# Row-sum copies of branch b issued at weight quarters 16, 20 and 24 instead of 25, 29 and 33, and one pair of row quarters requested two weight quarters later

## The reference, cut to what matters

```python
h = rmsnorm(x, p['norm_w']) * (1 + scale) + shift
proj = h @ p['w_in']
o_a, sfa, sba = gdn_branch(qkv, z_a, gate_cols, p, s_af, s_ab)     # branch a
o_b, sfb, sbb = lru_branch(x_b, z_b, p, s_bf, s_bb, col_major)     # branch b
pa = o_a @ p['w_proj_a']
pb = o_b @ p['w_proj_b']
g_a, g_b = jnp.split(jax.nn.sigmoid(h @ p['w_gate'] + p['b_gate']), 2, axis=-1)
mixed = (g_a * pa + g_b * pb) @ p['w_out']
return x + gate * mixed, ...
```

## Time and profile before

| | us |
|---|---|
| Median of 3 runs | 1464.38 (1463.67 to 1464.54) |
| The profiled execution, its own time | 1463.94 |
| Its span on the core | 1462.2 |
| PE busy | 1441.4 (99%) |
| DVE busy | 1140.8 (78%) |
| ACT busy | 872.8 (60%) |
| POOL busy | 457.2 (31%) |

### The profile page before, as it was taken

How to read it: one execution, slowest core, us unless ns; L and a number is a source line. 1 busy time by engine, 2 the same in 40 slices (tenths; PEclk the granted TensorE clock), 3 DMA queues, 4 the chain that set the end, 5 groups by cost and what they waited for, 6 DMA issues and landing times.

```text
span 1462.2 us, 29461 instructions
## 1 busy us (share of the span) xinstructions
PE 1441.4 (99%) x11640; PEld 1385.0 (95%) x11640; DVE 1140.8 (78%) x1983; ACT 872.8 (60%) x1836; POOL 457.2 (31%) x395
## 2 busy tenths in 40 slices
PE   8999999999999999999999999999999999999997
PEld 7899999999999999999899999999999999999886
DVE  5799898888989798888957766777666847888954
ACT  6574857667484756758357676556675564453311
POOL 3032322232332223233312122212224654656310
PEclk9999999999999999999999999999999999999999
DMA  9423133332413233432515686657868899747232
GB/s 315 123 70 123 31 79 112 75 110 62 140 48 78 96 75 109 122 123 80 162 40 144 197 218 150 140 180 198 172 171 267 263 276 253 224 151 237 107 130 101
DMA packets 177116, 210.26 MB, mean 144 GB/s; under 512 B 8681, under 2 KB 130386, under 8 KB 176978
## 3 DMA queue, kind: packets, MB, share of 16 engines
q1 hardware_dynamic: 162338, 171.74, 37.3%
q0 software_dynamic: 14352, 36.31, 12.3%
q10 hardware_dynamic: 288, 0.33, 0.1%
HBM read 178.83 MB, written 75.92 MB: 174 GB/s over the span
## 4 chain that ended last, share of the span: by engine, by line
PE 89%; DMA 4%; ACT 2%; DVE 2%; SPq 1%; issue 1%; POOL 1%; POOLq 0%; ACTq 0%; DVEq 0%
PE db L141 10%; PE db L143 9%; PE db L142 9%; PE mb L142 9%; PE mb L143 9%; PE mb L141 9%; PE mb L2604 4%; PE mb L2605 4%; PE mb L2606 4%; PE db L1409 3%; PE db L1381 2%; PE db L1425 2%; PE db L1398 2%; DMA m_w<-weight_sums 2%; PE db L1419 2%; PE db L1043 2%
## 5 line engine op out<-in xcount | busy, mean ns | idle before, releaser
L141 PE MATMUL db<-h_hi,w_hi 128*128 128x384 f32 x816 | 287.9, 353 | 0.2 <-DVE w_lo L1507 0.2
L143 PE MATMUL db<-h_hi,w_lo 128*128 128x384 f32 x816 | 274.5, 336 | 0.0
L142 PE MATMUL db<-h_lo,w_hi 128*128 128x384 f32 x816 | 274.5, 336 | 0.0
L2604 PE MATMUL mb<-h_hi,w_hi 128*128 128x288 f32 x616 | 182.5, 296 | 4.7 <-POOL w_lo L2309 4.7
L142 PE MATMUL mb<-h_lo,w_hi 128*128 128x384 f32 x552 | 185.5, 336 | 0.0
L141 PE MATMUL mb<-h_hi,w_hi 128*128 128x384 f32 x552 | 185.5, 336 | 0.0
L143 PE MATMUL mb<-h_hi,w_lo 128*128 128x384 f32 x552 | 185.5, 336 | 0.0
L2605 PE MATMUL mb<-h_lo,w_hi 128*128 128x288 f32 x616 | 182.0, 295 | 0.0
L2606 PE MATMUL mb<-h_hi,w_lo 128*128 128x288 f32 x616 | 182.0, 295 | 0.0
L141 PEld LDWEIGHTS db<-h_hi,w_hi 128*128 128x128 f32 x816 | 153.7, 188 | 4.1 <-DVE w_lo L1507 0.7
L142 PEld LDWEIGHTS db<-h_lo,w_hi 128*128 128x128 f32 x816 | 153.9, 189 | 0.0
(11 more groups left out here) (395 smaller groups left out, 3507.1 us busy)
## 6 DMA issues: line engine op xcount, KB each, us to landing
w<-in_w_in SPq DMA_DIRECT2D x48, 512.0 KB, 4.4
d_dt<-decay_rows SPq DMA_DIRECT2D x16, 576.0 KB, 7.0
d_qg<-decay_rows SPq DMA_DIRECT2D x16, 512.0 KB, 4.2
weight_sums<-in_w_proj_a POOLq DMA_DIRECT2D x8, 1024.0 KB, 10.2
weight_sums<-in_w_proj_b POOLq DMA_DIRECT2D x8, 1024.0 KB, 10.4
w<-weight_sums SPq DMA_DIRECT2D x23, 256.0 KB, 5.4
w<-in_w_gate SPq DMA_DIRECT2D x10, 512.0 KB, 4.5
m_w<-weight_sums SPq DMA_DIRECT2D x19, 256.0 KB, 7.1
```

The lines of the kernel that those rows point to most:

```text
L141: pe.matmul(out, hi, rhi, start=(k == 0), stop=False)
L142: pe.matmul(out, hi, rlo, start=False, stop=False)
L143: return pe.matmul(out, lo, rhi, start=False, stop=(last and stop))
L2604: pe.matmul(out, hi, rhi, start=(j == 0 and m not in BEHIND), stop=False, skip_group_check=True)
```

## The change

SP: the three copies of branch b's row quarters move from behind items 25, 29, 33 to behind items 16, 20, 24. POOL: the three accumulating transfers onto them move from n = 29, 33, 37 to n = 20, 24, 28. SP: the two row quarters of phase 5 are requested behind item 11 (`last_of[3]`) instead of behind item 9 (`first_of[3]`). SP: the wait for and the two small stores of `new_bf` and `new_bb` move from behind item 11 to behind item 30. PE, DVE and ACT run the same programs.

```diff
-                elif n == 11:
+                elif n == 30:
                     sp.wait_ge(S["nb"], 1)
                     for d, name in enumerate(("new_bf", "new_bb")):
                         sp.dma_start(A[name][0, 0].rearrange("(r p) -> r p", p=P), nb[d * H:(d + 1) * H, :]
                                      ).then_inc(S["nb_out"], 16)
-                if n in (25, 29, 33):
-                    copy_rows(2, ((n - 25) // 4,))
-                if n == first_of[3]:
+                if n in (16, 20, 24):
+                    copy_rows(2, ((n - 16) // 4,))
+                if n == last_of[3]:
                     quads_in(2, (5,))
                     other_in(5)
...
-                if n in (29, 33, 37):
-                    add_rows(2, (n - 29) // 4)
+                if n in (20, 24, 28):
+                    add_rows(2, (n - 20) // 4)
```

## The result

| | before | after |
|---|---|---|
| Median us | 1464.74 (22 runs, 1462.07 to 1468.94) | 1467.17 (22 runs, 1465.66 to 1470.00) |
| Ratio of the runs | | 1.0013, 95% interval 1.0007 to 1.0019 |
| Span of the profiled execution | 1462.2 | 1464.4 |

What follows compares the result with a forecast made beforehand. PE, busy 1441.4 of 1462.2 us, was taken as the bound. Full DMA engines make w = 26 10.1 us late, less 5.2 us of old losses: +4.9, 1463.94 to 1468.8, 1469.3 by the median, forecast 1469; 8-in-10 range 1461 to 1474.

Steps and rivals of the forecast that it cites:

- The first loss: Seventh stage, w = 9 and 10: PE's waits for POOL's low parts go, 2.3 + 0.44 = 2.7 us.
- The price of DVE's wait: w = 11 to 14: PE waits for DVE, delayed by phase 5's row quarters; 0 to 2.7 us, 1.5 taken, outside the sum.
- The accumulates: Two accumulating transfers ahead of the raw weights of items 25 to 27: 6.4 us of all engines each, 12.9 in all.
- The copies: Two copies moved into the stretch 1144 to 1177: 3.0 us of all engines each (upper bound 4.1), 6.0 in all.
- The sum on the DMA engines: Up to item 27's second transfer: 1177 + 18.9 - 2.7 = 1193.2; with POOL's work w = 26 starts at 1195.5.
- the term for the pauses: Stretch 1144 to 1177 at share 0.95: pauses take up 5% of 33 us = 1.7 us of the added work.
- rather in front: Second accumulate mostly passes ahead of item 27's weights; half through would give 1192.9 instead of 1196.1, 1195.5 taken.
- What PE makes of it: w = 26 starts at 1195.5, 10.1 us late in absolute time whatever PE lost before, spread over w = 22 to 27.
- The third loss: w = 34: the 2.43 us wait goes; DMA share clearly lower from 1195 to 1215, at least 12 us of engine time gone.
- A: Queues catch up: item 26's low part made by 1187, all 5.2 us go less 0 to 2: 1460; chance 0.21.
- B: Loss only moves: second accumulate mostly behind item 27, item 26 ready 1188 to 1193, time 1462 to 1467; chance 0.15.
- C: DVE replaces the loss at w = 9 and 10: up to 2.7 us at w = 11 to 14, 1465 to 1467; chance 0.07.

Runs made afterwards that it cites:

- experiment 2: Kernel before with only phase 5's row quarters behind item 11 and the two small stores behind item 30; copies and accumulating transfers as before: ratio 0.9996 to before.
- experiment 5: Changed kernel plus 24 identity matmuls on PE ahead of weight quarter 22's wait: ratio 1.0019 to the kernel before.
- experiment 1: Kernel before with only branch b's copies and accumulating transfers sooner; phase 5's row quarters and the small stores as before: ratio 1.0022 to before, 3.2 us slower.
- experiment 3: Changed kernel with only the accumulating transfers back behind items 29, 33 and 37: ratio 0.9969 to the kernel before, 4.5 us faster.
- experiment 4: Changed kernel with branch b's three accumulating transfers as plain transfers of the same bytes, the sum left out: ratio 0.9985 to the kernel before.

## Why the prediction was right in direction and too large in size

**Forecast.** 1469 (+4.9) was forecast, 1467.17 measured, +1.9 by the ratio: slower, within the range, at well under half the size. By the prediction's own bound of 0.2% it counts as no change, to which it had given 0.22.

**The first loss (2.7 us goes).** Right, with no wait at w = 9 and 10. The price of DVE's wait, 0 to 2.7 us, was about right too: none in the changed kernel's profile, 2.9 us in experiment 2, and 2 us of waits in experiment 5, which has the changed kernel's programs but for the fillers at w = 22; so it differs between executions. That it doesn't enter the sum is shown by experiment 1, in which PE comes to w = 22 later and starts it at nearly the same time.

**The accumulates (6.4 us each).** Right: 6.2 us by experiment 3, and half of that as a plain transfer by experiment 4.

**The copies (3.0 us each).** Right by the stretch from 1176 to 1178 us above. Experiment 3 has all three sooner and loses nothing there.

**The sum on the DMA engines: the term for the pauses failed.** "Taken up by pauses: 5% of 33 us = 1.7" reads the share against 1.00. Full engines are recorded above that. Experiment 1 is the kernel in which PE waits for them at w = 26, and its item 27 has landed at 1190.85; its stretches until then are:

```profile
1140.00:1144.00 4.00, 4.00 (x33) 4.00 (x32) 4.00 (x6) 1.21 (x2) 2.92 (x2) 1.00 0.22 18
1144.00:1190.85 46.85, 44.25 (x331) 43.64 (x329) 28.00 (x41) 26.69 (x46) 20.52 (x16) 1.00 1.09 322
```

With 1.09 for full engines the 0.95 of before leaves (1.09 - 0.95) / 1.09 of 33 us = 4.2 us of pause, an estimate, 2.5 us more than the term had. The sum's 1193.2 for item 27's landing becomes 1190.7, against 1190.85 measured; what else is off in the sum cancels to within 0.2 us, and the runs don't take that apart. The earlier trace rows already had 1.04 for two full stretches. PE started w = 26 at 1193.39, not at 1195.5. This is most of the 3.0 us by which the forecast missed.

The other choice of the sum held: the second accumulate is "rather in front", and more than that. Its 528 packets have all started when item 27 has landed. The queues of experiment 1 (packets, MB, share), first from 1180 to 1190.85, then from 1182 to 1188, where both have work all the time:

```profile
q0 software_dynamic: 528, 1.18, 60.5%
q1 hardware_dynamic: 2927, 1.46, 51.0%
```

```profile
q0 software_dynamic: 433, 1.00, 90.4%
q1 hardware_dynamic: 442, 0.22, 17.3%
```

The Trainium skill, DMA: Bandwidth & Descriptors, section Queues, rings and completion order, has an engine take turns between queues packet by packet. The trace agrees: 433 packets of one queue beside 442 of the other. The prediction read 475 beside 993 in the earlier trace rows as a ratio of two, and that was a misreading of the window: in the kernel before, from 1209 to 1212 us and then from 1213 to 1214, the queues have

```profile
q0 software_dynamic: 227, 0.52, 92.2%
q1 hardware_dynamic: 226, 0.11, 19.2%
```

```profile
q1 hardware_dynamic: 520, 0.26, 86.5%
q0 software_dynamic: 14, 0.02, 10.1%
```

So about half of the 993 passed when the accumulate was all but done. While it runs, a 2304-byte packet of it passes for each 512-byte packet of the weights: about one weight transfer of 512 packets beside one accumulate. How many of these packets make one turn, the counts do not tell.

**What PE makes of it.** The bound in absolute time held: w = 26 starts 91.4 us behind the stage's first matmul in experiment 1 (1193.39 - 1101.97), and 91.3 in experiment 5 (1195.12 - 1103.87), with quite different waits before; no change stood at 88.1, and the forecast at 93.0 (1195.5 - 1102.49). Where the loss lies I had wrong: I spread it over w = 22 to 27, put nothing for the clock, and looked for 8 to 12 us of waits. The changed kernel has one wait of 4.6 us and 2.6 us of slow matmuls behind it. With these, PE needs w = 26 no sooner than the DMA engines allow: item 26's low part is ready at 1192.7, and PE, slowed, comes 0.4 us later. There POOL's sum of item 27 waited for PE (2.58 us, above) and not for its weights. So the size in the changed kernel is set at w = 22. PE reaches w = 26 there 90.7 us behind the first matmul; that this lies so near to the 91.4 us that item 27's weights allow is luck.

**The third loss goes.** Right, and experiment 3 beside experiment 2 shows that the copies' move does it. But the DMA share from 1192 to 1215 is 0.97, not "clearly lower": the third accumulate and the delayed requests fill it. A full stretch costs nothing by itself.

**The rivals.** A needed item 26 by 1187 and fell. B's mechanism (the second accumulate behind item 27) is not what happened, since the accumulate was through first; that the result lies at the upper end of B's stretch is luck. The first half of C, DVE's wait, came true in experiment 2. The upper end of the likeliest range, 1199.5, does not come out of the terms named beside it: 1196.1 and two copies at 1.1 us more each give 1198.3.

## What to carry to other kernels

Before moving a background transfer, read from the trace how long it holds all DMA engines (here an accumulating one held them twice as long as a plain one), and place the expensive one by itself: the copies could go forward, the accumulates could not, and splitting the pair, with phase 5's row quarters behind item 11, gave 4.5 us. Before counting pauses, read what share the engines show when they are full (here 1.04 to 1.09, not 1.00), and take the rate of two queues from a window in which both have work all the time. A loss upstream of a resource that is full in absolute time is not worth removing alone: experiment 1 puts it back and w = 22 starts at the same time. What phase 5's row quarters give in experiment 3 by themselves no run shows.

## What the runs showed of the hardware that I had not expected

- TensorE's granted clock fell to 0.50 behind a wait of 4.61 us and stayed there for about 6 us. Behind waits of 2.27 us before and 2.12 us in experiment 1 it stayed at 1.00; behind 1.95 us in experiment 2 and 2.46 in experiment 1 (w = 26) it fell for a shorter time, here the stretches of PE in experiment 2:

```profile
1217.00:1219.00 2.00, 1.93 (x10) 0.66 0.29 87
1219.00:1221.00 2.00, 2.00 (x10) 0.50 0.55 160
1221.00:1223.00 2.00, 2.00 (x17) 0.99 0.71 164
```

  With identity matmuls in place of a wait as long as that of the changed kernel it stayed at 1.00.
- While both DMA queues had work, they passed packet for packet though the sizes differed: 433 packets with 1.00 MB beside 442 with 0.22 MB in 6 us of experiment 1. So the queue with the large packets had 90.4% of the engines' time.
- A request on SP can take long by itself; here it did in a stretch in which the DMA engines were full. SP's timeline of the changed kernel has the third copy's request at 4.36 us, where the copies' requests in the earlier trace rows took 0.49 and 0.65 us. It stands behind item 22's request (1159.30), so it did not delay item 22.

```profile
1167.84 4.36 SPq L2091 DMA_DIRECT2D row_sums<-branch_b  x1
```
